# Down weights of experts 1 to 31 issued by GpSimd instead of SyncE, in a one-core top-4-of-32 expert kernel

## The chip, the cores and the metric

One Trainium2 chip, one core of it. The kernel is one launch, and the time is the device time of that launch in microseconds (us). The kernel before took 1030.18 us (median of 3 runs, 1029.1 to 1030.41); the execution that was profiled took 1029.9 us, of which the profile's span is 1028.2 us.

## The reference, cut to what matters

The kernel computes one layer on x of 256 tokens by 1024 features, in float32: a mixer (an input projection, two short convolutions, a gated linear recurrence, an output projection), a layer norm, an expert feed-forward part, and a second layer norm. The expert part takes nearly all the time:

```python
logits = (xt @ w_router + b_router)            # 256 x 32
top_v, top_e = lax.top_k(logits, 4)            # 4 of 32 experts for each token
gates = jax.nn.softmax(top_v)
# for each expert e, for the tokens that chose it:
h = xb @ w_gu[e] + b_gu[e]                     # w_gu[e]: 1024 x 2048, 8 MB
h_glu = jnp.minimum(h[:, :1024], 7.0)
h_lin = jnp.clip(h[:, 1024:], -7.0, 7.0)
act = h_glu * jax.nn.sigmoid(1.702 * h_glu) * (h_lin + 1.0)
y = act @ w_dn[e] + b_dn[e]                    # w_dn[e]: 1024 x 1024, 4 MB
# each token's sum over its 4 experts of gate * y, then a layer norm
```

Every expert is chosen by some token, so all 32 experts' weights, 12.6 MB each, have to be read once.

## The kernel before, in words

**Stages.** The first part (to about 130 us of the span) is the mixer, the first norm and the routing. Its weights and the first experts' weights are loaded meanwhile. Then the experts follow one after the other. The tokens of an expert are handled in blocks of 32 (`SLOTS`). There are 46 blocks in all; an expert here has one block or two. `bounds[e]`, computed on the device, is the number of blocks of all experts before e, and `blocks_before(e)` reads it into a register.

**A block on TensorE** (`expert_block`, line 875): the bias matmuls (L879), then the gate-up matmuls in four chunks `c` of two rows of tiles (L885), each chunk behind a wait for its weights (`gu_in[b][c]`) and each ended by `gu_used[c]`; the gather of the next block's rows (L835); the combining of the block before (L859); a transposition (L853); then, when VectorE has the activations ready (L669 to L677), the down matmuls in two halves `m` (L918), each behind a wait for its weights (`dn_in[m]`) and each ended by `dn_used[m]` (for the second half that semaphore is `y_ps`). A two-block expert runs this twice on the same weights.

**Buffers.** `gu_buf` holds the gate-up weights of two experts (`b` is 0 for even experts and 1 for odd ones), 8 MB each in four chunks of 2 MB. `dn_buf` holds the down weights of one expert, in two halves of 2 MB. The first half of expert 1 goes into other tiles that are free by then (`dn_extra`, filled by `load_extra`). So gate-up weights can run ahead of TensorE by a whole expert and more, while a half of the down weights of expert e can be begun only when the last block of expert e-1 has used that half.

**The order of the loads.** All weights are started by SyncE (`block.sync`), in program order, on SyncE's own DMA queue. From expert 3 on a loop runs over pairs of experts and issues, in turn: the two halves of down weights of an odd expert (`stream_dn`, L272 to L275, with the issue itself on L270), the four chunks of the next even expert's gate-up weights (`stream_gu`, L261 to L266), and the same for the next pair. Each issue stands behind a wait that its part of the buffer has been used by the last block that needs it. A wait holds up all that is behind it on SyncE. Behind the loop SyncE starts the two loads of the second norm's gains and biases (L294, L295), and then the four stores of the output (L299).

**GpSimd** (`block.gpsimd`) builds constants at the start, computes the first norm's reciprocal roots (L338), and then has nothing to do until the last norm's (L341).

Of the kernel before, what the change touches and what calls it, by code (L numbers as in the profile page):

```python
# [29 lines left out]
GROUPS = P // SLOTS  # L30
# [12 lines left out]
def trunk(nc, x, w_in, conv_w, lru_conv_w, lru_conv_b, w_rgate, b_rgate, w_igate, b_igate, lru_lambda, w_out,  # L43
# [6 lines left out]
    E = w_router.shape[2]  # L50
# [8 lines left out]
    GC = 4  # L59
# [6 lines left out]
    with ExitStack() as ctx:  # L66
# [3 lines left out]
        def sem(name):  # L70
            return ctx.enter_context(nc.semaphore(name))
# [108 lines left out]
        rx_in = [sem(f"rx_in{i}") for i in range(3)]  # L180
        gu_in = [[sem(f"gu_in{b}{c}") for c in range(GC)] for b in range(2)]
        dn_in = [sem(f"dn_in{c}") for c in range(DC)]
        gu_used = [sem(f"gu_used{c}") for c in range(GC - 1)] + [S["h_ps"]]
# [10 lines left out]
        def dn_chunk(c):  # L194
            return dn_buf[:, DK * c:DK * (c + 1), :].rearrange("p q n -> p (q n)")
# [9 lines left out]
        def _(sp):  # L205
# [3 lines left out]
            def load_dn(e, c):  # L209
                return sp.dma_start(dn_chunk(c), dn_src[e][:, DRUN * c:DRUN * (c + 1)]).then_inc(dn_in[c], 16)  # L210

# [55 lines left out]

            def stream_dn_chunk(e, c, used):
                sp.wait_ge(dn_used[c], used)
                sp.dma_start(dn_chunk(c), dn_src[bass.ds(e, 1)].rearrange("o p r -> p (o r)")[:, DRUN * c:DRUN * (c + 1)]).then_inc(dn_in[c], 16)  # L270

            def stream_dn(e):  # L272
                used = blocks_before(e)
                for c in range(DC):
                    stream_dn_chunk(e, c, used)  # L275

            stream_gu(2, 0, range(0, GC // 2))
            sp.wait_ge(S["x1_ok"], 2 * TH)
            load_extra(1)  # L280
            stream_gu(2, 0, range(GC // 2, GC))
            after_0 = blocks_before(1)
            stream_dn_chunk(1, 1, after_0)
            stream_dn_chunk(2, 0, after_0)
            stream_gu(3, 1, range(0, GC // 2))
            stream_dn_chunk(2, 1, blocks_before(2))
            stream_gu(3, 1, range(GC // 2, GC))
            with sp.Fori(2, E // 2) as pair:
                stream_dn(pair * 2 - 1)
                stream_gu(pair * 2, 0)  # L290
                stream_dn(pair * 2)
                stream_gu(pair * 2 + 1, 1)
            stream_dn(E - 1)
            sp.dma_start(late[:, 0, :], ln2_g[0:1, :].to_broadcast([P, D])).then_inc(S["ln2_in"], 16)  # L294
# [9 lines left out]
        def _(pool):  # L304
# [31 lines left out]
            for h in range(TH):  # L336
                pool.wait_ge(S["var_ok"], h + 1)
                nc.gpsimd.tensor_tensor(small[:, 374 + h:375 + h], small[:, 370 + h:371 + h], small[:, 380:381], ALU.pow).then_inc(S["rstd_ok"], 1)  # L338
            for h in range(TH):
                pool.wait_ge(S["fin_var"], h + 1)  # L340
                nc.gpsimd.tensor_tensor(small[:, 374 + h:375 + h], small[:, 370 + h:371 + h], small[:, 380:381], ALU.pow).then_inc(S["fin_rstd"], 1)  # L341
# [360 lines left out]
        def _(pe):  # L702
# [219 lines left out]

            def down_at(m, count):
                return dn_in[m], count, [dn_buf[:, DK * m + j, :] for j in range(DK)]

# [6 lines left out]

            down_0 = [down_at(m, 16) for m in range(DC)]
            expert_block(0, 1, 0, 16, down_0, first=True)
            pe.wait_ge(S["bounds_ok"], 1)
            end = pe.value_load(bounds[0:1, 1:2], min_val=1, max_val=MAXB)
            with pe.If(end > 1):
                with pe.Fori(1, end) as g:
                    expert_block(g, g + 1, 0, 16, down_0)
            expert(1, 1, 16, [(S["extra_in"], 16 * GROUPS, dn_extra), down_at(1, 32)])  # L940

            def pair_of_experts(pair):
                for b in range(2):
                    e = pair * 2 + b
                    expert(e, b, (pair + 1) * 16, [down_at(0, e * 16), down_at(1, (e + 1) * 16)])

# [37 lines left out]
```

## Time and profile before

| what | value |
|---|---|
| time, median of 3 runs | 1030.18 us (1029.1 to 1030.41) |
| the profiled execution | 1029.9 us |
| its span | 1028.2 us |
| TensorE matmul busy | 831.2 us (81%) |
| TensorE weight loads busy | 359.9 us (35%) |
| VectorE busy | 243.4 us (24%) |
| ScalarE busy | 73.1 us (7%) |
| GpSimd busy | 6.2 us (1%) |
| moved by DMA | 422.64 MB, mean 411 GB/s |

The shares of busy time belong to the whole span. In the strip of 40 slices of the page each digit is the busy share of one slice in tenths, `PEclk` the clock granted to TensorE in tenths, and `DMA` the mean busy share of the 16 DMA engines. The chain that ended last, the page's section 4, is 51% DMA of down weights into `dn_buf` and 40% TensorE.

### The profile page before, as it was taken

What the parts mean: (1) busy time and instruction counts of PE and PEld (TensorE: products, weight loads), DVE (VectorE), ACT (ScalarE), POOL (GpSimd) and SP (SyncE); (2) the same over time, 40 slices, a digit from 0 to 9 for tenths busy, and PEclk for the clock granted to TensorE, in tenths of its full rate; (3) what the DMA queues carried; (4) which work ended last, traced back from release to release, by engine and by line L of the source; (5) the groups of instructions that cost most, each with busy time, mean ns of one, the idle gap of its engine ahead of it and who ended that gap; (6) DMA issues with size and microseconds to landing.
All of it is one profiled execution on the core that took longest, in us unless ns stands there. A gap on an engine that the chain in (4) does not pass through costs nothing.

```text
span 1028.2 us, 20061 instructions
## 1 busy us (share of the span) xinstructions
PE 831.2 (81%) x8403; PEld 359.9 (35%) x8404; DVE 243.4 (24%) x674; ACT 73.1 (7%) x173; POOL 6.2 (1%) x24
## 2 busy tenths in 40 slices
PE   9999879897659999986699977656966987876963
PEld 8885434333213334332233422222311322321321
DVE  2473712221112122211122211111201211211114
ACT  1030100000000000000000000000000000000000
POOL 1000000000000000000000000000000000000000
PEclk9999989999889999998899997898978899978988
DMA  9988699999999999999999999999999999999995
GB/s 333 413 334 327 267 426 424 428 428 428 429 428 429 428 429 428 428 428 428 429 425 428 428 428 428 428 428 430 429 428 428 428 428 428 428 428 428 428 426 214
DMA packets 38730, 422.64 MB, mean 411 GB/s; under 512 B 5884, under 2 KB 6328, under 8 KB 14264
## 3 DMA queue, kind: packets, MB, share of 16 engines
q1 hardware_dynamic: 36320, 421.93, 97.4%
q10 hardware_dynamic: 2392, 0.44, 0.2%
q8 instruction: 14, 0.23, 0.1%
q14 instruction: 4, 0.03, 0.0%
HBM read 421.31 MB, written 1.05 MB: 411 GB/s over the span
## 4 chain that ended last, share of the span: by engine, by line
DMA 51%; PE 40%; DVE 6%; issue 2%; DVEq 0%; ACT 0%; SPq 0%; POOL 0%; POOLq 0%
DMA dn_buf<-in_w_down_dram 51%; PE ps L885 14%; PE ps L918 13%; PE ps L722 5%; PE ps L765 3%; PE ps L879 2%; PE ps L739 1%; DVE act_t L677 1%; DVE lin L672 1%; DVE lin L675 1%; DVE glu L669 1%; DVE lin L670 1%; PE ps L714 0%; PE ps L798 0%; PE ps L753 0%
## 5 line engine op out<-in xcount | busy, mean ns | idle before, releaser
L885 PE MATMUL ps<-gu_buf,rows_t 128*32 128x512 f32 x2944 | 379.4, 661 | 112.6 <-DMA gu_buf<-in_w_gate_up_dram 112.6
L885 PEld LDWEIGHTS ps<-gu_buf,rows_t 128*32 128x32 f32 x2944 | 96.5, 116 | 383.4 <-issue 205.3
L918 PE MATMUL ps<-dn_buf,act_t 128*32 128x256 f32 x2912 | 175.0, 386 | 42.6 <-DMA dn_buf<-in_w_down_dram 34.3
L669 DVE TENSOR_SCALAR glu<-ps 128x256 f32<-128x256 f32 x46 | 19.5, 424 | 624.3 <-PE ps L885 624.3
L918 PEld LDWEIGHTS ps<-dn_buf,act_t 128*32 128x32 f32 x2912 | 90.2, 110 | 114.0 <-DMA dn_buf<-in_w_down_dram 46.0
L879 PE MATMUL ps<-turned,bias_sel 128*32 128x512 f32 x368 | 53.0, 649 | 25.0 <-issue 24.8
L407 ACT ACTIVATE sig<-glu 128x256 f32<-128x256 f32 x46 | 19.2, 417 | 560.9 <-DVE glu L669 560.9
L722 PE MATMUL ps<-turned,gu_buf 128*128 128x256 f32 x256 | 55.6, 379 | 0.0
L835 PE MATMUL ps<-xs,onehot 128*32 128x256 f32 x736 | 53.0, 409 | 1.4 <-DVE onehot L656 1.4
L859 PE MATMUL ps<-mix,back 32*128 32x256 f32 x736 | 53.7, 406 | 0.5 <-ACT mix L411 0.5
L722 PEld LDWEIGHTS ps<-turned,gu_buf 128*128 128x128 f32 x256 | 48.6, 190 | 6.6
L835 PEld LDWEIGHTS ps<-xs,onehot 128*32 128x32 f32 x736 | 26.4, 121 | 46.0 <-issue 37.1
L859 PEld LDWEIGHTS ps<-mix,back 32*128 32x128 f32 x736 | 34.0, 189 | 22.0 <-issue 19.8
L664 DVE TENSOR_SCALAR gated<-onehot,gates 128x128 f32<-128x128 f32 x92 | 22.2, 284 | 74.1 <-issue 74.1
L411 ACT COPY mix<-ps 128x256 f32<-128x256 f32 x46 | 17.1, 372 | 203.0 <-PE ps L918 203.0
L677 DVE STREAM_TRANSPOSE act_t<-lin 128x256 f32<-128x256 f32 x46 | 29.6, 644 | 1.6
L656 DVE TENSOR_SCALAR onehot<-slot_iota,block_base,places 128x128 f32<-128x128 f32 x92 | 27.8, 344 | 7.2 <-DVE gated L664 7.2
L765 PE MATMUL ps<-gu_buf,mix 128*128 128x512 f32 x64 | 28.0, 593 | 0.0
L879 PEld LDWEIGHTS ps<-turned,bias_sel 128*32 128x32 f32 x368 | 9.6, 114 | 43.4 <-issue 41.3
L409 ACT COPY back<-ps 128x256 f32<-128x256 f32 x46 | 17.1, 372 | 72.8 <-PE ps L853 72.8
L853 PE MATMUL ps<-ident,gated 128*128 128x128 f32 x92 | 20.1, 300 | 0.0
L672 DVE SCALAR_TENSOR_TENSOR lin<-lin,glu 128x256 f32<-128x256 f32 x46 | 19.5, 425 | 1.6
(182 smaller groups left out, 263.8 us busy)
## 6 DMA issues: line engine op xcount, KB each, us to landing
gu_buf<-in_w_gate_up_dram SPq DMA_DIRECT2D x128, 2048.0 KB, 29.5
dn_buf<-in_w_down_dram SPq DMA_DIRECT2D x63, 2048.0 KB, 13.5
gu_buf<-in_w_in_dram SPq DMA_DIRECT2D x4, 2048.0 KB, 18.4
gu_buf<-in_w_out_dram SPq DMA_DIRECT2D x2, 2048.0 KB, 15.6
xs<-in_x_dram SPq DMA_DIRECT2D x2, 512.0 KB, 3.8
gu_buf<-in_w_in_dram SPq DMA_DIRECT2D x2, 512.0 KB, 6.8
gu_buf<-in_w_in_dram SPq DMA_DIRECT2D x1, 1024.0 KB, 9.4
late<-in_ln_g_dram SPq DMA_DIRECT2D x2, 512.0 KB, 20.1
```

The costliest lines, as they stand in the source:

```text
L656: ins = V.tensor_scalar(onehot[:, h], slot_iota[:], base, column(h), ALU.add, ALU.is_equal)
L664: ins = V.tensor_scalar(gated[:, h, :], onehot[:, h].rearrange("p j s -> p (j s)"), gates[:, h, bass.ds(e, 1)], None, ALU.mult)
L669: V.tensor_scalar(glu[:], half(HB, 0), SWIGLU_LIMIT, None, ALU.min).then_inc(S["glu_ok"], 1)
L672: V.scalar_tensor_tensor(lin[:], lin[:], 1.0, glu[:], ALU.add, ALU.mult).then_inc(S["scaled_ok"], 1)
L677: V.transpose(act_t[:], in_blocks(lin[:])).then_inc(S["act_t_sb"], 1)
L722: ins = T.matmul(half(banks[c // 2], c % 2), w_piece[:, piece_slot[i], k, P * c:P * (c + 1)], turned[:, k, :], start=(k == 0), stop=(k == ...
L765: return T.matmul(ps[:, 2 * h + c, :], mix[:, k, P * h:P * (h + 1)], w_out_v[:, n, 512 * c:512 * c + 512], start=(n == 0), stop=(n == KT - 1))
L835: ins = T.matmul(ps[SLOTS * j:SLOTS * (j + 1), Y0, 0:QF], onehot[:, h, 0, :], xs[:, h, QF * j:QF * (j + 1)], start=(h == 0), stop=(h == TH ...
L859: ins = T.matmul(ps[:, j, QF * h:QF * (h + 1)], stationary[SLOTS * j:SLOTS * (j + 1), P * h:P * (h + 1)], moving[SLOTS * j:SLOTS * (j + 1) ...
L879: T.matmul(ps[SLOTS * j:SLOTS * (j + 1), HB, :], bias_sel[:, j, :], b_gu, start=True, stop=False)
L885: ins = T.matmul(ps[SLOTS * j:SLOTS * (j + 1), HB, :], rows_t[:, k, :], gu_buf[:, b, k, :].rearrange("p (two n) -> p two n", two=2)[:, :, ...
L918: ins = T.matmul(ps[SLOTS * j:SLOTS * (j + 1), YB, 0:QF], act_t[:, DK * m + q, :], weights[q][:, QF * j:QF * (j + 1)], start=(m == 0 and q ...
```

## The change

The down weights of experts 1 to 31 are no longer issued by SyncE but by GpSimd, from its own program and on its own queue. GpSimd issues them in the order of the experts, each half behind the same wait for `dn_used` as before. On SyncE the gate-up chunks now follow one another with nothing in between. Expert 0's down weights stay on SyncE and get semaphores of their own (`dn_first`), so the counts that TensorE waits for go down by 16. SyncE now waits for the landing of the last half of expert 31 before it starts the second norm's gains and biases, which it did not before.

```diff
+        dn_first = [sem(f"dn_first{c}") for c in range(DC)]
         dn_in = [sem(f"dn_in{c}") for c in range(DC)]
...
             def load_dn(e, c):
-                return sp.dma_start(dn_chunk(c), dn_src[e][:, DRUN * c:DRUN * (c + 1)]).then_inc(dn_in[c], 16)
+                return sp.dma_start(dn_chunk(c), dn_src[e][:, DRUN * c:DRUN * (c + 1)]).then_inc(dn_first[c], 16)
...
-            def stream_dn_chunk(e, c, used):
-                sp.wait_ge(dn_used[c], used)
-                sp.dma_start(dn_chunk(c), dn_src[bass.ds(e, 1)].rearrange("o p r -> p (o r)")[:, DRUN * c:DRUN * (c + 1)]).then_inc(dn_in[c], 16)
-
-            def stream_dn(e):
-                used = blocks_before(e)
-                for c in range(DC):
-                    stream_dn_chunk(e, c, used)
-
-
             stream_gu(2, 0, range(0, GC // 2))
             sp.wait_ge(S["x1_ok"], 2 * TH)
             load_extra(1)
             stream_gu(2, 0, range(GC // 2, GC))
-            after_0 = blocks_before(1)
-            stream_dn_chunk(1, 1, after_0)
-            stream_dn_chunk(2, 0, after_0)
-            stream_gu(3, 1, range(0, GC // 2))
-            stream_dn_chunk(2, 1, blocks_before(2))
-            stream_gu(3, 1, range(GC // 2, GC))
+            stream_gu(3, 1)
             with sp.Fori(2, E // 2) as pair:
-                stream_dn(pair * 2 - 1)
                 stream_gu(pair * 2, 0)
-                stream_dn(pair * 2)
                 stream_gu(pair * 2 + 1, 1)
-            stream_dn(E - 1)
+            sp.wait_ge(dn_in[1], 16 * (E - 1))
             sp.dma_start(late[:, 0, :], ln2_g[0:1, :].to_broadcast([P, D])).then_inc(S["ln2_in"], 16)
...
+            pool.wait_ge(S["bounds_ok"], 1)
+
+            def stream_dn_chunk(e, c, src, used):
+                pool.wait_ge(S["bounds_ok"], 1)
+                pool.wait_ge(dn_used[c], used)
+                pool.dma_start(dn_chunk(c), src[:, DRUN * c:DRUN * (c + 1)]).then_inc(dn_in[c], 16)
+
+            def blocks_before(e):
+                return pool.value_load(bounds[0:1, bass.ds(e, 1)], min_val=1, max_val=MAXB)
+
+            after_0 = blocks_before(1)
+            stream_dn_chunk(1, 1, dn_src[1], after_0)
+            stream_dn_chunk(2, 0, dn_src[2], after_0)
+            stream_dn_chunk(2, 1, dn_src[2], blocks_before(2))
+            with pool.Fori(3, E) as e:
+                used = blocks_before(e)
+                for c in range(DC):
+                    stream_dn_chunk(e, c, dn_src[bass.ds(e, 1)].rearrange("o p r -> p (o r)"), used)
...
-            def down_at(m, count):
-                return dn_in[m], count, [dn_buf[:, DK * m + j, :] for j in range(DK)]
+            def down_at(m, count, landed=dn_in):
+                return landed[m], count, [dn_buf[:, DK * m + j, :] for j in range(DK)]
...
-                    expert(e, b, (pair + 1) * 16, [down_at(0, e * 16), down_at(1, (e + 1) * 16)])
+                    expert(e, b, (pair + 1) * 16, [down_at(0, (e - 1) * 16), down_at(1, e * 16)])
```

How the instructions now stand is best seen at two places. The first is SyncE's loop over pairs of experts, the first of its two halves (an odd expert's down weights, then the next even expert's gate-up weights). Before:

```order
L270 ISA [waits dn_used0]
L270 DMA dn_buf<-in_w_down_dram 128x4096
L270 ISA [waits y_ps]
L270 DMA dn_buf<-in_w_down_dram 128x4096
L265 ISA [waits gu_used0]
L265 DMA gu_buf<-in_w_gate_up_dram 128x4096
L265 ISA [waits gu_used1]
L265 DMA gu_buf<-in_w_gate_up_dram 128x4096
```

And the same loop of the change, from its start (`h_ps` is the `gu_used` of the last chunk):

```order
L266 ISA [waits gu_used0]
L266 DMA gu_buf<-in_w_gate_up_dram 128x4096
L266 ISA [waits gu_used1]
L266 DMA gu_buf<-in_w_gate_up_dram 128x4096
L266 ISA [waits gu_used2]
L266 DMA gu_buf<-in_w_gate_up_dram 128x4096
L266 ISA [waits h_ps]
L266 DMA gu_buf<-in_w_gate_up_dram 128x4096
```

The gate-up chunks of an expert no longer stand behind a wait for the down matmuls of another, and the down halves no longer stand behind gate-up chunks.

The second place is GpSimd's program, up to its end, where the last norm's roots are. Before:

```order
L333 TENSOR_SCALAR scaled_ident<-ident 128x128 [waits ident_ok]
L334 MEMSET act_t 128x128
L335 MEMSET small 128x2
L338 TENSOR_TENSOR small<-small 128x1 [waits var_ok] x2
L341 TENSOR_TENSOR small<-small 128x1 [waits fin_var] x2
```

And in the change, from the loop over experts 3 to 31 to the last norm's roots:

```order
L337 UNCONDITIONAL_BRANCH
L337 ISA
L331 TENSOR_LOAD bounds
L331 ISA x2
L328 ISA [waits dn_used0,bounds_ok]
L328 DMA dn_buf<-in_w_down_dram 128x4096
L328 ISA [waits y_ps,bounds_ok]
L328 DMA dn_buf<-in_w_down_dram 128x4096
L337 REGISTER_ALU
L337 COMPARE_AND_BRANCH
L343 TENSOR_TENSOR small<-small 128x1 [waits fin_var] x2
```

Three loads before the loop and two in each of its 29 turns, 61 in all, now stand on GpSimd between the first norm's roots and the last norm's.

## Rows read from the trace of the kernel before

**Rows 1.** The page: slices of the span, and its DMA queues.

```profile
PEclk9999989999889999998899997898978899978988
DMA  9988699999999999999999999999999999999995
GB/s 333 413 334 327 267 426 424 428 428 428 429 428 429 428 429 428 428 428 428 429 425 428 428 428 428 428 428 430 429 428 428 428 428 428 428 428 428 428 426 214
q1 hardware_dynamic: 36320, 421.93, 97.4%
```

**Rows 2.** Busy time in stretches: us, engines, PEclk, DMA share, GB/s.

```profile
90.00:95.00 5.00, 5.00 (x13) 2.27 (x12) 0.00 (x0) 0.00 (x0) 0.00 (x0) 1.00 1.03 435
146.00:1012.00 866.00, 693.52 (x7626) 260.51 (x7618) 168.79 (x491) 51.87 (x134) 0.00 (x0) 0.92 1.01 428
```

**Rows 3.** Waits, whole span: total us, times, longest us.

```profile
SPq L270 <- PE ps L918: 713.5, 60, 39.4
PE ps L885 <- DMA gu_buf<-in_w_gate_up_dram: 112.6, 56, 3.4
PE ps L918 <- DMA dn_buf<-in_w_down_dram: 34.3, 28, 3.0
```

**Rows 4.** The chain that ended last, in order of time: start us, us, what.

```profile
322.75 13.26 DMA dn_buf<-in_w_down_dram
336.05 1.93 PE ps L918 x32
337.99 0.86 PE ps L879 x8
338.84 6.91 PE ps L885 x64
...
348.26 3.70 PE ps L918 x64
...
352.24 13.14 DMA dn_buf<-in_w_down_dram
...
440.23 13.27 DMA dn_buf<-in_w_down_dram
...
516.63 7.03 PE ps L885 x64
...
587.62 12.67 DMA dn_buf<-in_w_down_dram
```

**Rows 5.** The page: DMA issues, KB each, median us from issue to landing.

```profile
gu_buf<-in_w_gate_up_dram SPq DMA_DIRECT2D x128, 2048.0 KB, 29.5
out_dram<-xs SPq DMA_DIRECT2D x4, 256.0 KB, 2.0
```

**Rows 6.** DMA queues from 19 to 25 us: packets, MB, share of 16 engines.

```profile
q1 hardware_dynamic: 1026, 2.07, 94.2%
q10 hardware_dynamic: 1026, 0.13, 14.9%
```

**Rows 7.** TensorE in order of time, expert 18: start, us, line, tiles, count [idle before].

```profile
610.12 1.92 PE L885 MATMUL ps<-gu_buf,rows_t 128*32 128x512 f32 x16 [1.45 <-DMA gu_buf<-in_w_gate_up_dram]
619.92 3.64 PE L885 MATMUL ps<-gu_buf,rows_t 128*32 128x512 f32 x16 [1.89 <-DMA gu_buf<-in_w_gate_up_dram]
```

**Rows 8.** All engines in order of time, expert 31 and the end.

```profile
984.26 2.06 SPq L270 DMA_DIRECT2D dn_buf<-in_w_down_dram  x2
...
1003.15 1.92 PE L885 MATMUL ps<-gu_buf,rows_t 128*32 128x512 f32 x16 [1.42 <-DMA gu_buf<-in_w_gate_up_dram]
...
1006.86 0.64 DVE L677 STREAM_TRANSPOSE act_t<-lin 128x256 f32<-128x256 f32 x1
...
1012.97 1.94 PE L918 MATMUL ps<-dn_buf,act_t 128*32 128x256 f32 x32 [2.89 <-DMA dn_buf<-in_w_down_dram]
1014.98 0.37 ACT L411 COPY mix<-ps 128x256 f32<-128x256 f32 x1 [7.18 <-PE ps L918]
...
1016.68 1.42 DVE L530 BATCH_NORM_STATS2 small<-ps 128x6 f32<-128x256 f32 x4 [8.74 <-PE ps L859]
```

More of the change, by code:

```diff
@@ L930, in expert @@
                     expert_block(g, g + 1, b, loads, down)
-            down_0 = [down_at(m, 16) for m in range(DC)]
+            down_0 = [down_at(m, 16, dn_first) for m in range(DC)]
             expert_block(0, 1, 0, 16, down_0, first=True)
@@ L939, in _ @@
                     expert_block(g, g + 1, 0, 16, down_0)
-            expert(1, 1, 16, [(S["extra_in"], 16 * GROUPS, dn_extra), down_at(1, 32)])
+            expert(1, 1, 16, [(S["extra_in"], 16 * GROUPS, dn_extra), down_at(1, 16)])
             def pair_of_experts(pair):
```

## The prediction, made before the change was run

> **What bounds the kernel now.** I read the strip of slices first, then the stretches, the waits, and the chain of waits. The strip shows the DMA engines full from the sixth slice on, at 428 GB/s in nearly every slice, whatever TensorE does [rows 1]; over the 866 us from 146 to 1012 us the mean is 428 GB/s too [rows 2]. At that rate a half of 2.097 MB takes 4.9 us and an expert's 12.58 MB take 29.4 us. TensorE waits 112.6 us for gate-up weights and 34.3 us for down weights [rows 3]. SyncE waits 713.5 us on L270 for the down matmuls [rows 3], with gate-up chunks queued behind it, but this costs nothing: a gate-up chunk lands 29.5 us after its issue [rows 5], so the queue holds a whole expert's worth and never runs dry. The chain shows how close it is. In a run of two-block experts a load of down weights is started at 322.75 us, lands 13.26 us later, then come half a down step of 1.93 us and a second block of 14.0 us (337.99 to 348.26 + 3.70 us), and the next load starts at 352.24 us [rows 4]. That circle is 29.5 us, the time of an expert's bytes. Of the 13.26 us, 9.8 are the two halves themselves; only 3.4 us are gate-up bytes ahead of them. So DMA and the circle of the single down buffer take the same time here, with nothing to spare.
>
> **What the change removes.** SyncE's wait. As the engines are already full, nothing is gained by gate-up chunks issued earlier, and bytes are the same. The end can move by three things only: the rate, idle time of the DMA engines, and what follows the last landing.
>
> **What it adds: a second queue beside the first.** Until now down halves stood in one queue, behind the few gate-up bytes that were needed sooner, ahead of those needed later. Now the next gate-up chunks flow beside them. Where the trace has two queues at work (ScalarE's small loads beside SyncE's, 19 to 25 us), both moved 1026 packets, one to one, though one moved 2.07 MB and the other 0.13 MB [rows 6]. The gate-up and down halves both have runs of 16 KB per partition (4096 numbers), so one to one is half the rate each.
>
> Take a run of two-block experts, and X as the end of the down matmuls of expert e-1. I take 3 us from a release to the first byte. The nearest row is a store on SyncE's queue, 2.0 us to landing with 0.6 us of bytes in it [rows 5], so 1.4 us is the low end; for GpSimd, no row shows it, and I allow 6 us at the high end. The first half is released 1.9 us before X, so down bytes flow from X + 1.1. Gate-up weights of e+1 may start once the second block of e-1 has read chunk 0, about 11.6 us before X, so with SyncE's delay at X - 9.7; by X + 1.1 they have moved 10.8 us x 0.428 = 4.6 MB, and 3.8 MB are left. At half rate each these take 17.6 us, to X + 18.7; 0.4 MB of down weights are left and take 1.0 us. The second half lands at X + 19.7 instead of X + 13.3. With the 1.9 us and the 14.0 us behind it the circle is 35.7 to 35.9 us instead of 29.4, and for some 6.4 us of it nothing is left to load: expert e+2's gate-up weights wait for the second block of e, which waits for these down weights. That is the new loss: idle DMA.
>
> How often? The first two experts of a run are covered by what gate-up had loaded ahead. The chain has five two-block experts in a row (down loads from 279 us on, of which rows 4 show 322.75 to 440.23, four circles of 29.4 us), and three in a row between 516.63 and 587.62 us, where no DMA stands in the chain [rows 4]; the others come alone or in a pair. A one-block expert has a circle of about 24 us and gives the lag back. So 3 + 1 = 4 circles lose 6.4 us: 26 us. I stepped both queues through experts 1 to 31 with these durations (block 14.1 us, 0.6 us between experts), and got four idle stretches of 6.5 us and one of 0.6. The same steps with one queue put the last landing of before at 1011.3 us; it was at 1012.9 [rows 8].
>
> **The end.** In the steps with two queues the last gate-up chunk lands 4 us before the last down half, so TensorE ends 4.0 us after the last landing instead of 1.9: +2.2 us. The second norm's parameters are now issued after that landing, 2.5 us of bytes and about 2 us of delay; VectorE needs them some 3.7 us after the last down half's landing (1012.97 to 1016.68 [rows 8]), later here by the 2.1. They arrive about with the sums: 0 to +1 us. GpSimd's roots stand behind its last issue, long done: nothing.
>
> **The clock.** TensorE now waits about 8 us for the second half in such circles. Behind waits the granted clock falls (to 1.2 from 2.4 GHz: the 16 rows of a chunk take 3.64 instead of 1.92 us [rows 7]). A slow start of the second block costs 0 to 1.7 us in each of the four circles; I take 0.5: 2 us.
>
> **GpSimd's issue.** On the path is only the 3 us above, bounded by 1.4 and 6 us; my steps give 26 us in all for the low end and 39 for the high one. 
>
> **Rivals.**
> *GpSimd's queue gets more than half.* If its eight 16 KB runs per DMA engine go as one unit against single ones of SyncE's queue, it gets 8 parts of 9. Down halves then land some 12 us after X, nearly when wanted, and no DMA engine idles. But the last thing to land is gate-up chunk 3 of expert 31, at 1012.9 us. Before, that chunk was begun at 1003.15 us, activations were ready at 1007.50, so down matmuls could start 4.5 us after it, and take 3.7 us: 8.2 us to the end of down against 2.0 us now (1012.97 to 1014.98) [rows 8]. +6.2 us: 1036 us. For it: nothing in the rows; against it: one to one in rows 6. The Trainium skill, "DMA: Bandwidth & Descriptors", section "Queues, rings and completion order", says that a DMA engine goes round its queues by whole packets, typically of 9 to 17 descriptors. Rows 6 agree on the going round, but count one record against one. By the rule with 8 runs and a completion as one packet it is this rival, 1036, by rows 6 it is 1061. A share of 0.6 lies between (about 1045).
> *GpSimd's queue gets less than half*, as if its runs were cut smaller. Then down weights always land last, and after each landing the engines idle: 3.0 us with one block (1.9 + 1.1), 6.4 with two. 46 blocks over 32 experts make 14 of the latter: 16 x 3.0 + 14 x 6.4 = 138 us at most, about 100 in my steps for shares of 0.2 to 0.35: 1130 us. Nothing in the profile speaks for smaller runs.
> *Two queues are faster than one.* If the second fills gaps of the first, the rate could be 435 GB/s, as in the stretch from 90 to 95 us [rows 2]. The 371 MB of those 866 us would take 852, 14 less; with the end's +6.2 the time is 1022 us. It needs down weights to get more than half as well, for otherwise the idle stretches eat it. Against it: 428 GB/s stands unmoved in every slice, with the DMA share at 1.01 [rows 2].
> *The change doesn't do what it says:* a queue served strictly behind the other would make down weights later still, the second rival; a partly better rate that pays for the tail alone leaves 1030.
>
> **How the numbers follow.** One to one: 0.52, 1061. More than half: 0.28, 1036 to 1048. Less than half: 0.10, 1130. Faster: 0.06, 1022. No change: 0.04. What a measurement can tell from no change here is 0.2%, 2 us. Faster 0.06, same 0.04, slower 0.90. The range, 1032 to 1085, holds the first two cases and the high end of the issue's delay, and leaves out the others.
>
> **What would show it.** The strip should have slices under 400 GB/s near 390, 425, 460 and 610 us; TensorE's wait for down weights should rise from 34 us to over 120, and that for gate-up fall. A down load's time to landing should be about 20 us in runs. In the first rival the strip stays at 428, TensorE's waits stay near the old sum, and the last wait is for gate-up weights, not down. The mechanism is wrong if packets of both queues are not one to one where both are at work, and the theory as a whole if the time is under 1032.

## The result, and the profile after

The changed kernel takes 1087.81 us (median of 4 runs, 1085.62 to 1089.54) against 1029.99 us for the kernel before (median of 4 runs, 1029.1 to 1030.41). The ratio is 1.0555, with an interval of 1.0537 to 1.0573. So it is slower by 57.8 us; 31 were forecast, and the time lies 3 us above the range.

The page of the changed kernel, its strip of slices, its queues, the two groups of matmuls, and the issues of the two kinds of expert weights:

```profile
PEclk9999989889889889889989987977898698988888
GB/s 338 417 266 337 335 427 428 412 318 375 425 432 425 377 298 430 271 282 430 429 426 432 356 281 433 428 430 426 431 425 430 428 429 429 428 429 427 430 425 166
...
q1 hardware_dynamic: 27536, 294.00, 64.7%
q0 software_dynamic: 8784, 127.93, 27.7%
...
L887 PE MATMUL ps<-gu_buf,rows_t 128*32 128x512 f32 x2944 | 348.0, 623 | 58.6 <-DMA gu_buf<-in_w_gate_up_dram 58.6
L920 PE MATMUL ps<-dn_buf,act_t 128*32 128x256 f32 x2912 | 211.6, 446 | 156.6 <-DMA dn_buf<-in_w_down_dram 150.2
...
gu_buf<-in_w_gate_up_dram SPq DMA_DIRECT2D x128, 2048.0 KB, 26.0
dn_buf<-in_w_down_dram POOLq DMA_DIRECT2D x61, 2048.0 KB, 15.2
```

Against the strip of before [rows 1], in which every slice from the sixth to the 39th is at 424 to 430 GB/s, there are now holes in the 9th and 10th slice, from the 14th to the 18th (the 16th apart), and in the 23rd and 24th. A slice is 27.2 us, so these are the stretches near 218 to 272, 354 to 489 and 598 to 652 us. Elsewhere from the sixth slice on, up to the end, no slice but the 8th (412) is under 425. TensorE's wait for down weights rose from 34.3 to 150.2 us, and that for gate-up weights fell from 112.6 to 58.6 [rows 3].

The stretches of the changed kernel, in the columns of [rows 2]:

```profile
146.00:1068.00 922.00, 693.87 (x7564) 268.18 (x7560) 166.00 (x484) 51.12 (x132) 31.85 (x59) 0.87 0.95 402
390.00:399.00 9.00, 3.47 (x32) 1.44 (x32) 1.09 (x4) 0.00 (x0) 0.00 (x0) 0.79 0.91 390
399.00:406.00 7.00, 6.75 (x68) 2.58 (x72) 0.00 (x0) 0.37 (x1) 0.00 (x0) 0.78 0.00 0
406.00:415.00 9.00, 8.74 (x114) 3.74 (x110) 3.13 (x9) 0.79 (x2) 0.00 (x0) 1.00 0.98 393
730.00:1012.00 282.00, 198.36 (x2084) 73.84 (x2088) 45.94 (x134) 14.15 (x37) 9.71 (x18) 0.83 1.01 429
```

The same 371 MB now take 922 us at a mean of 402 GB/s instead of 866 at 428. From 399 to 406 us not a byte moves; from 730 us on the engines are full again at 429 GB/s. The loss is idle time of the DMA engines in certain places, and no lower rate. Where I go through the single transfers of this trace, there are seven stretches of over 2 us between 146 and 1010 us without any: from 238.9 us (8.9 us long), 366.2 (2.3), 398.8 (7.6), 436.6 (9.1), 476.0 (8.2), 602.5 (3.6) and 636.4 (8.2). That is 47.9 us; before has none.

The chain of waits of the changed kernel, one circle of a two-block expert: start us, us, what:

```profile
379.42 19.79 DMA dn_buf<-in_w_down_dram
...
399.25 3.31 PE ps L920 x32
402.57 0.86 PE ps L881 x8
403.43 6.92 PE ps L887 x64
...
412.86 3.70 PE ps L920 x64
...
417.25 19.75 DMA dn_buf<-in_w_down_dram
```

The load of the second half now takes 19.8 us where it took 13.3 [rows 4], and the circle, from issue to issue, 37.8 us (417.25 - 379.42) where it took 29.5. Within it are 3.31 us of down matmuls that took 1.93 us. Until TensorE has read the first chunk of gate-up weights in the second block, at 405.4 us, no chunk of expert e+2 can be started, as the prediction had it. The timeline of the changed kernel shows the issues (L266 is SyncE's gate-up, L328 GpSimd's down):

```profile
399.25 3.31 PE L920 MATMUL ps<-dn_buf,act_t 128*32 128x256 f32 x32 [4.15 <-DMA dn_buf<-in_w_down_dram]
...
405.37 5.46 SPq L266 DMA_DIRECT2D gu_buf<-in_w_gate_up_dram  x4
...
415.53 0.54 POOL L328 DMA_DIRECT2D dn_buf<-in_w_down_dram  x1 [35.57 <-PE ps L920]
...
417.25 0.54 POOL L328 DMA_DIRECT2D dn_buf<-in_w_down_dram  x1 [1.18 <-PE ps L920]
```

And its DMA queues (packets, MB, share of 16 engines), first from 415.6 to 419 us, just behind the first of those down issues, then from 419.4 to 428 us:

```profile
q1 hardware_dynamic: 104, 1.44, 99.1%
```

```profile
q0 software_dynamic: 121, 1.98, 53.7%
q1 hardware_dynamic: 120, 1.70, 46.3%
```

Where both queues work they move packets one for one (121 to 120), as forecast; 16 of the 120 are packets under 512 B, which come where a load ends, and they take a turn too. The counts alone would also fit engines that serve a group of rows of each queue in turn. The single transfers of this trace rule that out: from 420 to 423.5, 424.8 to 427.8 and 429.6 to 433 us, all 214 rows behind which a next one can be found on the same engine have one of the other queue next, so each engine changes queue after every row. But in the first 3.5 us after GpSimd's issue no packet of its queue has moved.

The end of the changed kernel, on several engines in order of time:

```profile
1050.74 0.54 POOL L328 DMA_DIRECT2D dn_buf<-in_w_down_dram  x1 [17.46 <-PE ps L920]
1056.47 3.64 PE L920 MATMUL ps<-dn_buf,act_t 128*32 128x256 f32 x32 [6.45 <-DMA dn_buf<-in_w_down_dram]
...
1060.85 0.54 POOL L328 DMA_DIRECT2D dn_buf<-in_w_down_dram  x1 [9.56 <-PE ps L920]
1061.24 7.04 PE L887 MATMUL ps<-gu_buf,rows_t 128*32 128x512 f32 x64
...
1068.35 0.34 SPq L278 DMA_DIRECT2D late<-in_ln_g_dram  x1
...
1070.76 3.66 PE L920 MATMUL ps<-dn_buf,act_t 128*32 128x256 f32 x64 [0.17 <-DVE act_t L679]
1074.49 0.37 ACT L413 COPY mix<-ps 128x256 f32<-128x256 f32 x1 [3.49 <-PE ps L920]
```

The last down half has landed at 1068.3 us, where SyncE's new wait ends; before, it had at 1012.9 [rows 8]. TensorE is done with the last down half at 1074.4, 6.1 us after it, where before it was 1.9 us. So the 59.5 us between the two spans are 55.4 us of later landing and 4.2 us of a longer tail. (Medians of the runs differ by 57.8; this execution is 1.7 us above its median.) At the end TensorE isn't behind the last load of down weights: expert 31's gate-up matmuls could only start when expert 30's down matmuls, kept waiting until 1056.47, were done.

### The profile page after: what moved, and what is told of

Same layout as the page of the kernel before. It is cut to its first block, busy times and chain, and to the rows that moved or that the text cites. A ratio compares the mean times of both kernels' runs of the same rounds, so it can differ in the third digit from the quotient of the medians.

```text
span 1087.7 us, 20214 instructions
## 1 busy us (share of the span) xinstructions
PE 834.1 (77%) x8403; PEld 368.7 (34%) x8404; DVE 243.1 (22%) x674; ACT 73.0 (7%) x173; POOL 39.5 (4%) x86
## 4 chain that ended last, share of the span: by engine, by line
DMA 47%; PE 42%; DVE 5%; another core or an unknown queue 3%; issue 3%; DVEq 0%; ACT 0%; POOLq 0%; SPq 0%
DMA dn_buf<-in_w_down_dram 29%; DMA gu_buf<-in_w_gate_up_dram 17%; PE ps L887 16%; PE ps L920 13%; PE ps L724 5%; PE ps L767 3%; PE ps L881 2%; PE ps L741 1%; DVE act_t L679 1%; DVE lin L677 1%; DVE lin L674 1%; DVE glu L671 1%; DMA gu_buf<-in_w_in_dram 1%; DVE lin L672 1%
## 5 line engine op out<-in xcount | busy, mean ns | idle before, releaser
L887 PE MATMUL ps<-gu_buf,rows_t 128*32 128x512 f32 x2944 | 348.0, 623 | 58.6 <-DMA gu_buf<-in_w_gate_up_dram 58.6
L920 PE MATMUL ps<-dn_buf,act_t 128*32 128x256 f32 x2912 | 211.6, 446 | 156.6 <-DMA dn_buf<-in_w_down_dram 150.2
L920 PEld LDWEIGHTS ps<-dn_buf,act_t 128*32 128x32 f32 x2912 | 100.4, 124 | 249.6 <-DMA dn_buf<-in_w_down_dram 164.0
L881 PE MATMUL ps<-turned,bias_sel 128*32 128x512 f32 x368 | 58.1, 709 | 20.4 <-issue 20.4
L328 POOL DMA_DIRECT2D dn_buf<-in_w_down_dram x61 | 33.2, 544 | 915.8 <-PE ps L920 915.8
## 6 DMA issues: line engine op xcount, KB each, us to landing
dn_buf<-in_w_down_dram POOLq DMA_DIRECT2D x61, 2048.0 KB, 15.2
gu_buf<-in_w_out_dram SPq DMA_DIRECT2D x2, 2048.0 KB, 15.2
```

The source lines that it names most:

```text
L328: pool.dma_start(dn_chunk(c), src[:, DRUN * c:DRUN * (c + 1)]).then_inc(dn_in[c], 16)
L881: T.matmul(ps[SLOTS * j:SLOTS * (j + 1), HB, :], bias_sel[:, j, :], b_gu, start=True, stop=False)
L887: ins = T.matmul(ps[SLOTS * j:SLOTS * (j + 1), HB, :], rows_t[:, k, :], gu_buf[:, b, k, :].rearrange("p (two n) -> p two n", two=2)[:, :, ...
L920: ins = T.matmul(ps[SLOTS * j:SLOTS * (j + 1), YB, 0:QF], act_t[:, DK * m + q, :], weights[q][:, QF * j:QF * (j + 1)], start=(m == 0 and q ...
```

## The experiments

Two things had to be found out: whether the mechanism is the forecast one (packets one for one, circle of the down buffer), and why it costs nearly twice the forecast. Edits are against the changed kernel unless said; ratios are to the kernel before.

**Gate-up rows of 4 KB.** If sharing is by packets, the share can be set by their size.

```diff
-  sp.dma_start(gu_chunk(b, c), gu_src...[:, GRUN * c:GRUN * (c + 1)])
+  for r in range(4):      # 1024 numbers of each partition at a time
+      sp.dma_start(gu_chunk(b, c)[:, 1024 * r:1024 * (r + 1)], gu_src...)
-  pe.wait_ge(gu_in[b][c], loads)
+  pe.wait_ge(gu_in[b][c], loads * 4)
```

> The changed kernel, with each 2 MB gate-up chunk loaded as four DMAs whose rows are 4 KB per partition; the down loads of GpSimd keep their 16 KB rows. Theory 1 (the two queues are served packet for packet, so the packet sizes set the shares): the down loads get 16 parts of 20 while both run, a pair of halves lands about 12 us after its issue, no DMA engine idles in the runs of two-block experts, and what is left is the later end behind the last gate-up chunk: 1034 to 1042 us. Theory 2 (a load issued by GpSimd is slow in itself, whatever runs beside it): unchanged, about 1088 us.

Measured: 1072.49 us, ratio 1.0403 [1.037, 1.0436]. Its queues from 408 to 414 us, its strip, its longest wait on TensorE, its down issues, and its window from 146 to 1010 us:

```profile
q0 software_dynamic: 141, 2.05, 80.5%
q1 hardware_dynamic: 137, 0.50, 20.5%
```

```profile
GB/s 335 403 299 342 290 416 421 407 416 421 412 417 415 417 401 392 416 363 414 416 412 413 391 420 416 418 412 416 419 414 416 410 428 406 422 411 416 416 416 107
```

```profile
PE ps L890 <- DMA gu_buf<-in_w_gate_up_dram: 155.7, 26, 11.7
```

```profile
dn_buf<-in_w_down_dram POOLq DMA_DIRECT2D x61, 2048.0 KB, 11.3
```

```profile
146.00:1010.00 864.00, 654.72 (x7315) 255.79 (x7310) 162.30 (x473) 49.93 (x129) 30.12 (x56) 0.89 1.01 412
```

Packets stay one for one (141 to 137), so bytes go four to one. A down half lands 11.3 us after its issue (median) instead of 15.2. The idle stretches are gone but for 1.7 us, and TensorE's wait has moved to gate-up weights, as in the first rival. The expected time, 1034 to 1042 us, was missed all the same, for a reason that no theory had: with 4 KB rows the full engines move 412 GB/s, not 428. For the 371 MB that is 34 us of the 42.6 lost here.

**Rows of 8 KB**, once for gate-up alone and once for down alone.

> The changed kernel, with each gate-up chunk loaded as two DMAs with rows of 8 KB; down loads keep rows of 16 KB, so by packet-for-packet service they get two thirds while both run. In between the changed kernel and the run with 4 KB rows in its idle stretches: four or so, of 6 us, where the changed kernel has seven. My steps give 20 us less than for equal packets, 1065 to 1072 us with a small loss of rate. If packet sizes do not set the shares: 1088 us or more.

Measured: 1076.93 us, ratio 1.0449 [1.0426, 1.0472]; idle stretches of 0.9 to 6.9 us, 23.4 in all up to 1010 us. The time is 5 us above the upper end of what was expected; the stretches halved.

```diff
-  pool.dma_start(dn_chunk(c), src[:, DRUN * c:DRUN * (c + 1)])
+  for r in range(2):      # 8 KB rows of down weights, gate-up's stay 16 KB
+      pool.dma_start(dn_chunk(c)[:, 2048 * r:2048 * (r + 1)], src[...])
```

> The changed kernel, with each down half loaded by GpSimd as two DMAs with rows of 8 KB, while gate-up rows stay 16 KB: by packet-for-packet service the down loads get one third. Theory 1: loads of down weights take up to 29 us while both run, every expert's circle is too long, and my steps give 69 us more than for equal packets: 1150 to 1165 us. If packet sizes do not set the shares: 1088 to 1095 us.

Measured: 1149.25 us, ratio 1.1162 [1.1144, 1.1181], with 14 idle stretches of 6.1 to 8.1 us over the whole expert part (1 us under what was expected). The share of the down queue sets the loss, in both directions, and packets set the share. This one is in effect the prediction's rival "less than half"; its price of 1130 was 19 us low.

**One block for each expert**, in the changed kernel and in the one before. These two leave out the tokens of an expert beyond its first 32.

```diff
-  link(V.tensor_scalar(nb_i, cnt, 1.0, SLOTS - 1.0, ALU.max, ALU.add))
+  link(V.tensor_scalar(nb_i, cnt, 1.0, SLOTS - 1.0, ALU.min, ALU.add))
```

> The changed kernel, with one block for every expert (tokens of an expert beyond the first 32 are left out, so 32 blocks instead of 46). The bytes loaded are the same. Theory 1: a one-block expert's circle is about 26 us, under the 29.4 us of an expert's bytes, so no DMA engine idles though both queues still share packet for packet; only the later end is left: 1034 to 1042 us. Theory 2 (each load by GpSimd costs time in itself, 61 of them): most of the 58 us stays, over 1070 us.

> The kernel before, with one block for every expert (tokens beyond the first 32 of an expert are left out), as the reference for the changed kernel with one block, 1035.5 us. Theory 1: bound by the same bytes, 1028 to 1031 us, so that what the two queues cost there is the later end behind the last gate-up chunk, 5 to 7 us.

Measured: 1035.51 us, ratio 1.0051 [1.0034, 1.0067], for the change with one block; 1030.53 us, 0.9997 [0.9988, 1.0007], for the kernel before with one block. No DMA engine idles, and the changed kernel's queues run at the full rate from 146 to 1010 us:

```profile
146.00:1010.00 864.00, 525.47 (x5168) 182.65 (x5160) 113.38 (x330) 34.83 (x90) 31.80 (x59) 0.80 1.01 428
```

Without second blocks 5.0 us are left of the 57.8. They are the tail, seen in the timeline of the one-block change:

```profile
1010.26 3.64 PE L887 MATMUL ps<-gu_buf,rows_t 128*32 128x512 f32 x16 [6.36 <-DMA gu_buf<-in_w_gate_up_dram]
1013.27 0.34 SPq L278 DMA_DIRECT2D late<-in_ln_g_dram  x1
...
1016.46 3.66 PE L920 MATMUL ps<-dn_buf,act_t 128*32 128x256 f32 x64
1020.19 0.37 ACT L413 COPY mix<-ps 128x256 f32<-128x256 f32 x1 [3.25 <-PE ps L920]
```

The last gate-up chunk comes late, and gate-up, activations and a whole down step follow: TensorE's last down matmul ends at 1020.1 instead of 1014.9 us [rows 8]. The prediction had priced that in a rival, at 6.2 us.

**Everything on GpSimd's queue**, in the order of before. If loads of GpSimd are slow in themselves, this is slow.

```diff
   # GpSimd's loop over pairs, in the old order; SyncE starts none of these
-  stream_gu(pair * 2, 0); stream_gu(pair * 2 + 1, 1)   # SyncE
+  stream_dn(pair * 2 - 1); stream_gu(pair * 2, 0)
+  stream_dn(pair * 2); stream_gu(pair * 2 + 1, 1)
```

> The kernel before, with its whole stream of gate-up and down weights from expert 2's gate-up on, in the old order, issued by GpSimd in place of SyncE: one queue again, but GpSimd's. Theory 1: nothing is shared, and the later first byte is hidden by what is queued ahead: 1029 to 1034 us. Theory 2 (GpSimd's loads are slow in themselves): at least as slow as the changed kernel, 1088 us or more, as three times as many loads are GpSimd's.

Measured: 1033.56 us, ratio 1.0032 [1.0019, 1.0045]. Its window and its queue:

```profile
146.00:1010.00 864.00, 683.28 (x7593) 256.80 (x7586) 168.02 (x489) 51.51 (x133) 94.10 (x175) 0.93 1.01 428
```

```profile
q0 software_dynamic: 26064, 379.60, 86.6%
```

GpSimd's queue carries 380 MB at the full 428 GB/s. In one queue and in the order of need the change of engine costs 3 us. The two queues are the cost.

**The queues swapped**: gate-up weights by GpSimd, down weights by SyncE.

```diff
-  sp.wait_ge(gu_used[c], used);   sp.dma_start(gu_chunk(b, c), ...)
+  sp.wait_ge(dn_used[c], used);   sp.dma_start(dn_chunk(c), ...)
-  pool.wait_ge(dn_used[c], used); pool.dma_start(dn_chunk(c), ...)
+  pool.wait_ge(gu_used[c], used); pool.dma_start(gu_chunk(b, c), ...)
```

> The two queues swapped: gate-up weights from expert 2 on issued by GpSimd, down weights of experts 1 to 31 by SyncE, each half as soon as it is free. The sharing is the same. If the late first byte of GpSimd's down loads is what made the loss larger than predicted: 12 to 20 us less than the changed kernel, 1068 to 1076 us. By my steps a bound circle is closed by the start of the next gate-up load, so what down loads win in it gate-up loads lose: 1082 to 1094 us. If GpSimd is no part of it at all, the same 1082 to 1094 us.

Measured: 1094.96 us, ratio 1.0625 [1.0607, 1.0643], 7 us more than the change. Its queues from 417.7 to 421.1 us, just after SyncE issued two down halves (at 417.6 and 419.3):

```profile
q0 software_dynamic: 109, 1.52, 104.7%
```

No packet of SyncE's queue has moved here either. So the late first byte is no matter of GpSimd. From the single transfers: with idle engines the first byte follows the issue by 1.0 us (SyncE in the change, at 405.4) or 1.2 us (GpSimd here). Beside a busy queue it follows by 3.6 to 3.9 us (GpSimd in the change), 3.4 to 3.7 us (SyncE here), and 3.4 to 3.7 us (ScalarE, below). In that time 83 to 100 packets of the other queue start, about six on each DMA engine. It isn't a fixed number of packets: in the runs above, GpSimd's first byte comes 3.6 to 3.8 us after the issue too, while 186 to 194 packets of 8 KB or 369 to 380 of 4 KB go first. In bytes that is 1.4 to 1.6 MB each time. Whether the engines hold so many bytes, or the delay is a time of its own, no run here tells apart. The swapped kernel's idle stretches add up to 55.4 us, so its 7 us stand in them.

**The down load begun later**, by four register loads ahead of each issue.

```diff
+  for _ in range(4):
+      pool.value_load(bounds[0:1, 0:1], min_val=0, max_val=MAXB)
```

> The changed kernel, with four register loads (some 2 us of GpSimd's time) between the release of each down half and its issue. It prices the late start of GpSimd's loads, 4.4 us from the release to the first byte in the changed kernel, where the prediction took 3. Theory 1: the start stands in each expert's circle until the gate-up buffers bound it; 2 us more bring the bound circles nearer to the start of each run and cost 10 to 18 us: 1098 to 1106 us. If loads are started early enough for their start not to matter: 1088 us.

Measured: 1095.27 us, ratio 1.0623 [1.0604, 1.0643], 3 us under what was expected. Behind a two-block expert the first half is issued 2.2 us later behind its release than in the change, and the second 3.3 us later, because it also stands behind the first one's register loads. So 7.5 us were paid for 2.2 to 3.3 us, or 2.3 to 3.4 us for each us of later start. The stretches where a run of two-block experts begins grew, from 2.3 to 7.9 us and from 3.6 to 7.9; of the five others none did.

**Down loads issued by ScalarE**, behind its last copy of an expert.

```diff
   # ScalarE, behind the blocks of expert e
+  for c in range(DC):
+      act.wait_ge(dn_used[c], end)
+      act.dma_start(dn_chunk(c), dn_src[e + 1]...).then_inc(dn_in[c], 16)
```

> The changed kernel, with the down loads of experts 1 to 31 issued by ScalarE on its own hardware queue, behind its copy of the last block's output, instead of by GpSimd. Theory 1 (sharing packet for packet makes the single down buffer's circle too long): the sharing stays, only the start of a load gets shorter by about 2 us, so 8 to 15 us are won: 1073 to 1080 us. Theory 2 (GpSimd's loads are slow in themselves): the loss goes, 1030 to 1040 us.

Measured: 1154.78 us, ratio 1.1222 [1.1183, 1.1261]. That is above all that was expected, by 75 us. In this form both halves are issued only when the whole buffer is free, so it loses the early start of the first half, and its wait on TensorE is spread over 57 steps:

```profile
PE ps L923 <- DMA dn_buf<-in_w_down_dram: 257.0, 57, 7.8
```

To see whether this is the cause, the same was done with GpSimd still issuing:

```diff
-  pool.wait_ge(dn_used[c], used)
+  pool.wait_ge(dn_used[1], used)
```

> The changed kernel, with the first down half waiting for the release of the second one too, so that both start when the whole buffer is free. In the changed kernel the first half is used, and released, 8 us before the second one has landed; ScalarE's loads in the earlier run had lost just that. Theory 1: one-block experts lose their shorter circle (4.4 + 19.6 + 3.7 us, against 18 to 26), nothing is given back between runs, and my steps give 60 to 75 us more: 1148 to 1163 us, as with ScalarE. If ScalarE's run was slow for a reason of ScalarE's queue: at most 10 us more, under 1098 us.

Measured: 1156.66 us, ratio 1.1213 [1.1187, 1.1239], with the same wait:

```profile
PE ps L920 <- DMA dn_buf<-in_w_down_dram: 252.9, 57, 8.2
```

So ScalarE isn't what was slow. The half-wise release, which the change leaves as it was, is worth 69 us here, because in experts with one block too the circle then becomes too long: its trace has 111 us of idle stretches, up to the end, where the change has 48.

**TensorE kept at its clock.** In the chain of the change the half behind the wait takes 3.3 us and not 1.9; the granted clock from 399 to 402.5 us is 0.56, so most of it ran at 1.2 GHz, the lower level, and not at 2.4. The remedy tried is matmuls without use, into a bank that is free, between the two down halves of an expert's first block:

```diff
+  if m == 1 and warm is not None:
+      with pe.If(prior == warm):
+          keep_warm(HB, 16)
```

> The changed kernel, with 16 matmuls of 128x128 by 128 into an unused bank between the two down halves of each expert's first block, where TensorE waits some 6 to 8 us for the second half; nothing else. Theory 1 with the clock as a part of the loss (the second half takes 3.7 us instead of 1.9 and the block behind it up to 1.4 us more, as TensorE comes out of the wait at the lower clock): both fall back, circles of two-block experts get 2 to 3 us shorter, and 15 to 24 us are won: 1064 to 1073 us. If the clock is of no account: 1088 us, or a little more.

> The changed kernel, with 7 matmuls between the two down halves of each expert's first block, where 16 had taken 3.8 to 4.4 us also from experts that need not wait. If the clock is a part of the loss, the idle stretches stay 2 us shorter than the changed kernel's 8 to 9 us and the cost to experts that don't wait halves: 1075 to 1086 us. If the gain of the clock is only taken from one place and paid in another: 1088 to 1094 us.

Measured: 1094.28 us, ratio 1.0634 [1.0601, 1.0667], with 16 of them, and 1089.51 us, 1.0577 [1.0557, 1.0597], with 7. Neither is faster than the change, so the gain that was expected of them (to 1064 to 1073, and to 1075 to 1086 us) isn't there. With 16 the second half takes 1.93 us again and the idle stretches within the run of five fall to 6.2 us. But the matmuls take 4 us in every expert, also where nothing waits, and the stretches at the start of the runs of five and of three grow from 2.3 to 6.5 and from 3.6 to 7.3 us: one-block experts give less of the lag back. To put them only where TensorE waits, its loop over pairs has to be written out; that alone is the control:

```diff
-  with pe.Fori(1, E // 2 - 1) as pair:
+  for pair in range(1, E // 2 - 1):
```

> The changed kernel, with TensorE's loop over pairs of experts written out, the control for the run beside it. Nothing in the circles changes: 1084 to 1092 us by either theory.

```diff
+  warm=first if e in (3, 4, 5, 8, 9, 10, 11, 12, 15, 16, 17, 22, 25, 27, 30) else None
```

> The run beside it with 14 matmuls between the down halves of the first block of those 15 experts alone in which TensorE waited over 6 us for the second half (3 to 5, 8 to 12, 15 to 17, 22, 25, 27, 30), so that no other expert pays for them. Theory with the clock: TensorE comes out of these waits at the full clock, 1.8 us at the second half and up to 1.4 us in the next block are won in each, and 15 to 22 us less than the control in all: 1066 to 1074 us. If the lower clock costs nothing in the end (a circle bound by the gate-up buffers gives it back elsewhere): within 5 us of the control.

Measured: 1102.31 us, ratio 1.0694 [1.0676, 1.0711], for the loop written out, and 1092.56 us, 1.0605 [1.0588, 1.0623], for the same with 14 matmuls in those 15 experts (the trace counts each of them twice, x28). TensorE in the same expert, without and with them:

```profile
403.21 3.26 PE L920 MATMUL ps<-dn_buf,act_t 128*32 128x256 f32 x32 [3.78 <-DMA dn_buf<-in_w_down_dram]
```

```profile
395.98 4.41 PE L711 MATMUL ps<-ident 128*128 128x128 f32 x28
400.33 1.93 PE L923 MATMUL ps<-dn_buf,act_t 128*32 128x256 f32 x32
```

The control missed what was expected of it: writing the loop out costs 14.5 us by itself, for which I have no shown cause (its trace has 50 packets on the instruction queue where the change has 14, and TensorE's wait for down weights is 167.4 us instead of 150.2). Between these two, which share that cost, the clock is worth 9.8 us; 15 to 22 were expected. Idle stretches, added up, go from 51.0 to 40.0 us. With the clock kept, the four in the middle of runs are 6.1 to 6.3 us long, about what the prediction had for them (6.4 to 6.5); the three where runs begin still add up to 15.3 us, where it had 0.6.

## Why the prediction was right about the mechanism and wrong about the size

**What held.** Bytes and rate are unchanged; the loss is idle DMA behind a second half that lands late. Packets go one for one where both queues work (121 to 120, and 141 to 137 with rows of a quarter of the size). A down load takes 19.8 us (forecast: "about 20"), TensorE's wait for down weights is 150.2 us ("over 120"), and the wait for gate-up fell. The holes named near 390, 425, 460 and 610 us are there, 9 to 26 us later (398.8, 436.6, 476.0 and 636.4). Without second blocks the loss isn't there. The rival "more than half" falls by the packet counts. The rule that it was built on, of the Trainium skill ("DMA: Bandwidth & Descriptors", "Queues, rings and completion order"), is seen here in its going round, but the engines change queue after every row of a partition, and not after the 9 to 17 descriptors that it gives as typical. The rival "two queues are faster" falls by 429 GB/s in the full stretches. GpSimd being locked out by VectorE, by the Trainium skill's "SBUF — State Buffer", "Who interferes with whom", doesn't show: its first bytes come 3.6 to 3.9 us after the issue, SyncE's 3.4 to 3.7.

**Where the missing time stands.** On the profiled execution the loss is 59.5 us and the sum was 30.8. Of the 28.7 us between them (the terms are rounded), 14.2 are the three idle stretches where runs begin (14.8 us, forecast 0.6). Another 5.1 are the four within runs (33.1 us; the forecast had 26, and 2 for the clock). The tail has 2.0, and 7.5 are DMA time lost outside full stops. So the largest thing that failed is the step "the first two experts of a run are covered"; the two steps that mis-sized a circle come next.

**Step "3 us from a release to the first byte".** It is 0.7 us from the release to the issue and 3.7 us to the first byte, 4.4 us. The row it rested on, a store of 2.0 us [rows 5], was measured on idle engines, where a load's first byte also takes 1.0 us here. Beside a full queue 1.4 to 1.6 MB of the other queue move first. In a circle as it was forecast this alone is little: the second half lands 20.5 us after the release (378.73 to 399.21), where the steps had 19.7, so 0.8 us. Over the whole kernel, 1.4 us more at the measured 2.3 to 3.4 us for each is 3 to 5 us, an estimate.

**Step "a slow start of the second block costs 0.5 us in each of the four circles: 2 us".** In the two kernels with the loop written out the clock costs 9.8 us. The second down half itself runs at the lower clock (3.3 to 3.6 us instead of 1.9), and it stands in the circle, in each of the experts where TensorE waits long for it (15 in that experiment). In the circle shown this is 1.4 us; with the 0.8 us above it makes the 37.8 us out of the 35.7 to 35.9 that were forecast. The prediction looked for the slow start in the block after it only, and in four circles.

**Step "the first two experts of a run are covered".** Three idle stretches stand where a run begins: 8.9 us at 238.9, 2.3 at 366.2 and 3.6 at 602.5, in all 14.8 us, where the steps had 0.6. The first stands behind a mere pair (experts 3 and 4), which the prediction took as covered. The runs show two things of them: a later start of the down loads makes the two others longer (7.9 us each), and keeping the clock doesn't take them away (15.3 us). By my stepping they need no cause of their own. With the two durations corrected (4.4 us; 1.8 us more for a late second half and 0.7 for the block behind it), the same stepping gives seven stretches in the same places, 50.9 us with the one at the end, and an end 52 us later than that of before. It gave 29 with the first durations. The two terms by themselves, at most 5 and 8 us, don't add up to that difference; by the stepping, each stretch that opens makes the next one start later and deeper, since the lead of gate-up, once gone, isn't won back within a run. That is stepped, not shown: why the lead that was to cover the first two experts of a run is smaller than forecast stays open in part.

**The tail.** 4.2 us instead of 2.2: the last gate-up matmuls waited for expert 30's down weights, which the steps didn't have. In the one-block kernels, where nothing else is lost, the tail is 5.0 us. The second norm's parameters and GpSimd's roots cost nothing that the trace shows, as forecast.

**What stays open.** The stepping ends at 52 of the 59.5 us. Two of the rest are the tail. The idle stretches are 47.9 us and the landing is 55.4 us later. Of the 7.5 us between them, 5.1 are the edges of those stretches, within 12 us on either side, in which only some of the 16 engines work (390 GB/s just before the one at 399 us, 393 just after it), and 1.2 lie in the last 23 us. No run changed these by themselves. No cause is shown either for the 7 us by which the swapped queues are worse than the change, or for the 14.5 us of the loop written out.

No variant beats the kernel before. Its engines are full at 428 GB/s, and all that an earlier issue can do is to change what lands first.

## What to carry to other kernels

A load that feeds a buffer with no second copy has to land and be used within the time that all bytes of a round take; here that was 29.5 us against 29.4, so any delay of it became idle DMA. When the engines are already full, a second queue doesn't start anything sooner: it takes the order of need out of your hands and shares packet for packet, by which the urgent load is held to half the rate when rows are equally long. Its first byte came 3.4 to 3.9 us after the issue here, whoever issued it. Before moving a load to another queue, write down its circle (delay to first byte beside a full queue, bytes at the shared rate, the work behind it at the clock that follows a wait) and compare it with the time of a round's bytes.

## What the runs showed of the hardware

- Two queues with work on the same engines took turns after every row of a partition, whether rows were of 16 KB on both (121 to 120 packets) or of 16 and 4 KB (141 to 137 packets, 2.05 to 0.50 MB).
- Time from issue to first byte depended on what the engines were doing far more than on who issued: 1.0 us (SyncE) and 1.2 us (GpSimd) when idle; 3.4 to 3.9 us for SyncE, ScalarE and GpSimd beside a full queue. 1.4 to 1.6 MB of the other queue went first, as 83 to 100 rows of 16 KB, 186 to 194 of 8 KB, or 369 to 380 of 4 KB.
- With all engines full, the kernel moved 428 GB/s with rows of 16 KB, on either queue, and 412 GB/s with gate-up rows of 4 KB (161 ns for one on its engine, against 613 ns for one of 16 KB in the change).
- GpSimd's queue carries large loads as well as SyncE's: 379.6 MB, with the mean of both at 428 GB/s, and the kernel took 3 us more than the one before.
- In the change, halves of 32 down matmuls behind waits of 4.0 to 7.9 us took 3.3 to 3.6 us (granted clock 0.50 from 437 to 440.2 us, around one of them), and 1.93 us in the runs where matmuls without use kept TensorE busy in that wait.
